# Sums of squares for the group norm: GpSimd adds two tiles, TensorE sums them over the partitions

## What is computed

```python
y = (y_diag + y_off).reshape(b, s, H, P) + xh * d_skip[:, None]
y = y.reshape(b, s, 1024) * silu(z)
yg = y.reshape(b, s, 4, 256)
yg = yg * rsqrt(mean(yg * yg, axis=-1, keepdims=True) + EPS)
y = yg.reshape(b, s, 1024) * norm_w
```

## Time and profile before

| | us |
|---|---|
| median of three runs | 1951.73 |
| lowest and highest | 1951.63, 1952.05 |
| the profiled execution | 1952.31 |
| its span | 1950.5 |
| TensorE busy | 1925.8 |
| VectorE busy | 1322.7 |
| ScalarE busy | 1101.4 |
| GpSimd busy | 166.3 |

### The profile page before, as it was taken

The page is one execution under the profiler, slowest core; times in us unless marked ns, Lnnn a source line. Parts: engine busy times, 40 slices in busy tenths (PEclk is TensorE's granted clock), DMA queues, the critical chain, the costliest instruction groups (busy, mean ns, idle before and its releaser), DMA issues.

```text
span 1950.5 us, 29009 instructions
## 1 busy us (share of the span) xinstructions
PE 1925.8 (99%) x11352; PEld 1661.3 (85%) x11352; DVE 1322.7 (68%) x2282; ACT 1101.4 (56%) x1852; POOL 166.3 (9%) x248
## 2 busy tenths in 40 slices
PE   9999999999999999999999999999999999999999
PEld 8878998887899988888987788888888897878887
DVE  5866976576697657556787875555555688886554
ACT  6666765476676554445567554444444566655442
POOL 1110222011012100000012200000000001210000
PEclk9999999999999999999999999999999999999999
DMA  8434556543455655555543355555555544345553
GB/s 300 139 105 141 190 182 234 182 139 112 140 170 188 197 181 193 185 187 176 175 157 107 108 178 189 185 183 191 180 189 187 182 153 150 100 132 183 189 184 123
DMA packets 90680, 329.83 MB, mean 169 GB/s; under 512 B 10032, under 2 KB 10416, under 8 KB 90288
## 3 DMA queue, kind: packets, MB, share of 16 engines
q1 hardware_dynamic: 90544, 327.98, 51.1%
HBM read 326.89 MB, written 1.05 MB: 168 GB/s over the span
## 4 chain that ended last, share of the span: by engine, by line
PE 88%; DVE 6%; ACT 4%; issue 1%; DMA 1%; SPq 0%; DVEq 0%; ACTq 0%
PE PS L83 85%; PE PS L86 3%; DVE WL L98 2%; ACT TMP L95 1%; DVE TMP L108 1%; ACT WH L92 1%; DVE SM L114 1%; DMA RAW<-wts 1%; ACT M L92 0%; ACT M L95 0%; SPq L80 0%; ACT TMP L92 0%; DVE X L98 0%; DVE SM L108 0%; DVE SM L98 0%
## 5 line engine op out<-in xcount | busy, mean ns | idle before, releaser
L98 DVE TENSOR_TENSOR WL<-RAW,WH 128x1024 fp32r<-128x1024 f32 (+1 forms) x609 | 745.6, 1230 | 476.3 <-ACT WH L92 469.8
L92 ACT ACTIVATE WH<-RAW 128x1024 fp32r<-128x1024 f32 (+1 forms) x609 | 641.3, 1057 | 533.5 <-PE PS L83 526.6
L83 PE MATMUL PS<-WH,GH 128*128 128x512 f32 (+1 forms) x1008 | 397.2, 394 | 4.9 <-DVE GL L98 4.7
L83 PE MATMUL PS<-WH,GL 128*128 128x512 f32 (+1 forms) x1008 | 388.5, 385 | 0.0
L83 PE MATMUL PS<-WL,GH 128*128 128x512 f32 (+1 forms) x1008 | 388.2, 385 | 0.0
L83 PE MATMUL PS<-WH,HH 128*128 128x512 f32 (+1 forms) x832 | 315.8, 380 | 0.0
L83 PE MATMUL PS<-WL,HH 128*128 128x512 f32 (+1 forms) x832 | 312.2, 375 | 0.0
L83 PE MATMUL PS<-WH,HL 128*128 128x512 f32 (+1 forms) x832 | 312.2, 375 | 0.0
L83 PE MATMUL PS<-GH,WH 128*128 128x256 f32 x928 | 264.5, 285 | 0.8 <-issue 0.4
L83 PE MATMUL PS<-GL,WH 128*128 128x256 f32 x928 | 262.6, 283 | 0.0
L83 PE MATMUL PS<-GH,WL 128*128 128x256 f32 x928 | 262.6, 283 | 0.0
(11 more groups left out here) (151 smaller groups left out, 2151.8 us busy)
## 6 DMA issues: line engine op xcount, KB each, us to landing
RAW<-wts SPq DMA_DIRECT2D x607, 512.0 KB, 4.1
M<-bias SPq DMA_DIRECT2D x4, 512.0 KB, 10.8
M<-bias SPq DMA_DIRECT2D x1, 2048.0 KB, 9.6
X<-x SPq DMA_DIRECT2D x2, 512.0 KB, 5.7
TMP<-mem SPq DMA_DIRECT2D x1, 1024.0 KB, 12.0
out<-X SPq DMA_DIRECT2D x4, 256.0 KB, 3.8
CST<-cst SPq DMA_DIRECT2D x1, 714.0 KB, 9.8
RAW<-wts SPq DMA_DIRECT2D x2, 256.0 KB, 5.9
```

The lines of the kernel that those rows point to most:

```text
L83: return Issued(self.eng and self.eng.matmul(o, l, r, start=first, stop=last, skip_group_check=share))
L92: return Issued(self.eng.activation(o, i, f, scale=scale))
L98: return Issued(self.eng and self.eng.tensor_tensor(o, a, b, op))
```

## The change

GpSimd gets three more instructions in each layer: behind gates 2, 4 and 6 it waits for the square of tile m - 1 and adds the two squares of group m / 2 - 1, in place in `y_sq(m - 2)`. `y_sums` of groups 0, 1 and 2 then waits for that addition (signal `paired`) and has two matmuls in place of four. Group 3 stays as it was.

```diff
-        gated = signal("gated")
+        gated, paired = signal("gated"), signal("paired")
...
                     ps = bank(("ys", L, g // 2))
-                    for q in range(2):
-                        m_ = 2 * g + q
-                        e.wait_ge(squared, ("y", L, m_))
+                    parts = (2 * g, 2 * g + 1) if g == 3 else (2 * g,)
+                    for m_ in parts:
+                        if g == 3:
+                            e.wait_ge(squared, ("y", L, m_))
+                        else:
+                            e.wait_ge(paired, ("y", L, g))
                         for t in range(2):
                             m = e.mm(ps[:, t * 2 + g % 2:t * 2 + g % 2 + 1],
                                      y_sq(m_)[:, t * 128:t * 128 + 128], cc(C_ONE, 1),
-                                     g % 2 == 0 and q == 0 and t == 0, q == 1, share=True)
+                                     g % 2 == 0 and t == 0, m_ == parts[-1], share=True)
                     m.then_inc(summed, ("y", L, g))
...
                     e.tt(y, y, Z[:, m, :], ALU.mult).then_inc(gated, ("yz", L, m))
+                    if m in (2, 4, 6):
+                        e.wait_ge(squared, ("y", L, m - 1))
+                        e.tt(y_sq(m - 2), y_sq(m - 2), y_sq(m - 1), ALU.add).then_inc(paired, ("y", L, m // 2 - 1))
```

## The result

| | before | after |
|---|---|---|
| median of 22 runs, us | 1952.05 | 1954.45 |
| lowest and highest | 1951.43, 1952.56 | 1953.41, 1957.47 |
| the profiled execution, its span | 1952.31, 1950.5 | 1955.51, 1953.7 |
| ratio of the times, 95% interval | | 1.0015, [1.0008, 1.0021] |

The change costs 2.4 us by the medians, 2.0 us between the fastest runs; 2.1 was forecast. It is slower, clear of no change; the interval of the ratio reaches from 0.08% to 0.21%, with the ratio itself under the 0.2% set as the bound. The slowest runs of the changed kernel lie 4 us over its fastest, where the kernel before spreads over 1.1 us.

The account below looks back on a forecast made before the run. TensorE was taken to bound the kernel. Per layer 0.76 (wait for addition 1) + 0.53 (VectorE late) - 0.25 (later sums) = +1.04 us, +2.1 us over two layers: 1953.8 us from 1951.7, range 1951.7 to 1956.8.

Parts of the forecast that it names:

- TensorE bounds, and the matmuls are on its path: TensorE busy 99% of the span; dropping two matmuls each for groups 0, 1, 2 gains 2.8 us if nothing waits.
- First place, group 1: Sums after head pair p = 5: TensorE waits for addition 1, queued behind gate 4; +0.76 us a layer.
- recorded sign: Between two groups of four one-column records after head pair p = 5, TensorE idle 1.7 to 2.3 us, released by GpSimd's addition.
- First place, group 0: Addition 0, itself hidden, collides with the masks of p = 4 and makes VectorE late: +0.53 us a layer.
- Second place: Later sums in each layer, before the last projection: 0.47 us less matmul, partly lost waiting for tile 7's square; -0.25 us.
- The sum: 0.76 + 0.53 - 0.25 = +1.04 us a layer, +2.1 us for two layers.
- The clock: Clock falls behind the first sums likelier in both layers; put at nothing, 0.42 us either way being inside the range.
- the first rival: Slower by falls of the clock: one uncovered fall in each layer gives 1956.8 us; chance 0.14, two uncovered falls 0.09.
- The second rival: No loss: gate 4 and addition 1 take turns with VectorE's instructions, group 1 ends +0.25 us, total 1951.7 us; chance 0.12.

Follow-up runs that it names:

- the additions alone: Kernel before plus the three GpSimd additions, written into a buffer nobody reads, TensorE still summing all squares: 1953.15 us against 1952.31.
- group 1 undone: The change with addition 1 taken back, group 1 summed from two squares again, additions 0 and 2 kept: 1951.67 us against 1952.31 for the kernel before.
- the wait filled: The change with three matmuls of constants between the sums of groups 0 and 1, so TensorE works meanwhile: 1953.70 us against 1951.86 for the kernel before.
- the matmuls alone: Kernel before without the matmuls on the second tile of groups 0, 1 and 2, and without additions: 1949.40 us against 1952.31.

## Why the prediction was right

- **TensorE bounds, and the matmuls are on its path.** 2.8 us worked out, 2.9 measured with nothing else changed. That they agree so closely is luck: the traces give 1.22 us a layer, and 0.4 us is a fall of the clock that went with the matmuls. The missing 0.2 us a layer are mostly the wait for the square of tile 7, which the forecast has as a term of its own, at the second place.
- **First place, group 1.** Right in mechanism and size: gate 4 at 2.58 us, the addition at 0.72 behind it, TensorE empty meanwhile. The empty stretch is 1.66 us from the end of group 0 at 0.117 us a record (1105.18 + 0.47) to 1107.31, and 1.7 was forecast; the row reads 1.53 because the last record is shown as busy for longer. The recorded sign, 1.7 to 2.3 us idle, is just missed at its low end. Undoing group 1 alone takes the loss away.
- **First place, group 0.** Right in size (masks at 1.56 us, addition at 1.05), but the way to TensorE was other than the prediction put it. It said head pair 4 is just in time and the lateness comes out at gate 4. It comes out at TensorE before that, at the decays of heads 12 and 13, which wait for banks that ScalarE frees. It counts once all the same: gate 4 is 0.5 us later, and so is TensorE when it comes to wait, so the stretch is 1.7 us and not 2.2. With the additions alone it is the whole cost.
- **Second place.** -0.25 us forecast, -0.45 measured (1119.74 to 1121.00 is 1.26 us, against 1.71). The wait for the square of tile 7 did not come, because TensorE arrived late: the fall of the clock had cost it 0.4 us since the decay of head 14 (11.89 us against 11.49), while VectorE went on. Where the clock did not fall, with group 1 undone and with the wait filled, this place takes 1.40 to 1.41 us: -0.30, with a wait in it, close to what was worked out.
- **The sum.** Without a fall the terms come to 1.32 - 0.30 = 1.02 us a layer, against 1.04 forecast; layer 1 with the wait filled has 1.03 (21.17 us from head pair 4 to the matmul behind the second sums, against 20.14 in layer 0 before). What the profiled execution has beyond that, and beyond the fall in layer 1 before, is the clock: its stretches are 21.41 and 22.84 us.
- **The clock.** It was put at nothing in the forecast and at 3 us in the first rival; it is in between. The falls cost 0.4 us in layer 0 of the profiled execution. In layer 1 the stretch from the decay to the second sums is 12.92 us against 11.91, and the second four records took 0.94 us instead of 0.54: 1.4 us more than before, for a fall of 7 us in place of 3.4. In layer 0 the wait behind the sums covers most of the fall, as was argued (3.4 us at half speed are 1.7 us of work); in layer 1 it covers about half of one twice as long. But 2 of 22 runs lie over 1956.8, the upper end given. This term is what makes the medians differ by 2.4 rather than by the 2.0 of the fastest runs. That 2.1 lies between the two owes something to chance, since the kernel before pays for a fall as well.
- **The second rival** fell as an account of the change: in the profiled execution gate 4 waited out the whole row in both layers. It did happen twice elsewhere, in layer 0 of the matmuls alone and of the wait filled, so among the change's other runs, which have no trace, it is not excluded.

## What to carry to other kernels

Work moved off the bounding engine gains only if its result is ready when that engine asks; here the move took a wait on a square, long done, and put one in its place on the last instruction of a queue that had a gate of another tile ahead of it. Ask of every added instruction what stands ahead of it on its engine, and of every wait whether the consumer can stand later: moving the sums of group 1 behind the next decay gave 2.25 us without any of the change (some 0.4 of it the clock), and moving both sums and addition 0 gave 4.15 with it. And an instruction nobody waits for can still cost, when it holds up an engine whose work is chained.

## What the runs showed of the hardware

- A GpSimd instruction with two SBUF operands, issued under a row of three VectorE instructions (WL and two masks), took 2.57 to 2.60 us against 0.72 to 0.74 alone. Of the 22 rows of gate 4 issued in this way (both layers of eleven traces), 20 are so; two took 1.64 and 1.65 us, each with the row of 2.58 us in the other layer of the same kernel: who gets the next turn is not settled by the program. "SBUF — State Buffer" of the Trainium skill says, under "SBUF: two separate sides", that whichever of the two starts first has the shared ports for its whole instruction while the other blocks; the durations agree with whole instructions, but gate 4 mostly stood behind three of them, not only the one that was running.
- The granted clock fell to 1.2 GHz behind the one-column matmuls even where TensorE had no gap between them (layer 1 before, 0.66 in its window). With 1.5 us without work among them it fell in both layers, for 3.4 and 6.8 us, and none of 22 runs has a mean clock of 1.000; 15 of the 87 runs of the kernel before that were timed beside the experiments have it. With that stretch filled ten of eleven have it, and with the sums of group 1, or of both groups, later all 44 of four kernels. These runs don't separate the gap from the number of one-column matmuls in one place.
